# Differential-attention units: the rotated rows of queries and keys come by transfers instead of products with a matrix, and the value projection is cut into half blocks

## The reference, cut to what matters

```python
def apply_partial_rope(x, cos, sin):
    half = ROT_DIM // 2                       # 8
    x1, x2, xp = x[..., :half], x[..., half:ROT_DIM], x[..., ROT_DIM:]
    return jnp.concatenate([x1 * c - x2 * s, x2 * c + x1 * s, xp], axis=-1)
...
u = rms_norm(h, g_mix[l]) @ w_in[l]
qa = u[..., ...].reshape(B, S, DA_HEADS, 2, HEAD_DIM)     # 4 heads, 2 components each
ka = ...; va = ...
qa = apply_partial_rope(qa, cos, sin)
ka = apply_partial_rope(ka, cos, sin)
ya = diff_attention(qa, ka, va, lam, g_subln[l], lam_init)
```

## Time and profile before

| | |
|---|---|
| Time, median of 3 runs | 2294.36 us (2291.03 to 2294.76) |
| Profiled execution, its own time | 2291.01 us, with a span of 2289.2 us |
| Mean granted TensorE clock | 0.995 of full speed |
| TensorE busy | 2214.7 us, 97% of the span |
| VectorE busy | 1377.4 us, 60% |
| ScalarE busy | 952.1 us, 42% |
| GpSimd busy | 700.9 us, 31% |
| Differential units | 72.6 us to about 310 us of the span |

### The profile page before, as it was taken

The page is one execution under the profiler, slowest core; times in us unless marked ns, Lnnn a source line. Parts: engine busy times, 40 slices in busy tenths (PEclk is TensorE's granted clock), DMA queues, the critical chain, the costliest instruction groups (busy, mean ns, idle before and its releaser), DMA issues.

```text
span 2289.2 us, 36425 instructions
## 1 busy us (share of the span) xinstructions
PE 2214.7 (97%) x14780; PEld 1752.0 (77%) x14780; DVE 1377.4 (60%) x1775; ACT 952.1 (42%) x1688; POOL 700.9 (31%) x436
## 2 busy tenths in 40 slices
PE   7999999998999999999999999999999999999997
PEld 4777776665788888788888888888676777778885
DVE  6777857778676544584574575323508376567554
ACT  4444457777544232354234334233416412363321
POOL 2312212121211213274564565322231133122231
PEclk9999999999999999999999999999999999999998
DMA  3211101113131001111111110112220011100022
GB/s 134 74 56 56 47 19 56 56 47 129 50 138 54 29 27 39 45 47 56 56 55 44 57 64 29 54 55 92 77 73 19 19 38 38 40 20 13 4 111 83
DMA packets 38555, 125.80 MB, mean 55 GB/s; under 512 B 3856, under 2 KB 4368, under 8 KB 37776
## 3 DMA queue, kind: packets, MB, share of 16 engines
q1 hardware_dynamic: 33936, 103.30, 13.3%
q10 hardware_dynamic: 4480, 20.49, 2.3%
HBM read 114.34 MB, written 8.91 MB: 54 GB/s over the span
## 4 chain that ended last, share of the span: by engine, by line
PE 86%; DVE 6%; ACT 4%; issue 3%; POOL 1%; DMA 0%; ACTq 0%; DVEq 0%; POOLq 0%
PE PS L184 23%; PE PS L186 22%; PE PS L185 22%; PE PS L2305 2%; PE PS L776 2%; PE PS L753 1%; PE PS L1212 1%; PE PS L938 1%; PE PS L903 1%; PE PS L920 1%; DVE arena L1024 1%; PE PS L312 1%; PE PS L1915 1%; PE PS L1775 1%; PE PS L1788 1%
## 5 line engine op out<-in xcount | busy, mean ns | idle before, releaser
L233 POOL TENSOR_TENSOR w_hi<-w_raw,const 128x1024 fp32r<-128x1024 f32 x77 | 152.0, 1974 | 1096.6 <-PE PS L184 985.9
L184 PE MATMUL PS<-u_r,w_hi 128*128 128x512 f32 x1184 | 477.6, 403 | 9.0 <-DVE h L590 3.1
L186 PE MATMUL PS<-u_r,w_lo 128*128 128x512 f32 x1184 | 462.1, 390 | 0.0
L194 POOL TENSOR_TENSOR w_lo<-w_raw,w_hi 128x1024 fp32r<-128x1024 f32 (+1 forms) x143 | 330.7, 2313 | 323.2 <-ACT w_hi L190 308.3
L185 PE MATMUL PS<-arena_r,w_hi 128*128 128x512 f32 (+1 forms) x888 | 331.9, 374 | 0.0
L184 PEld LDWEIGHTS PS<-u_r,w_hi 128*128 128x128 f32 x1184 | 222.5, 188 | 62.0 <-DVE h_r L194 6.5
L186 PEld LDWEIGHTS PS<-u_r,w_lo 128*128 128x128 f32 x1184 | 222.4, 188 | 47.7
L184 PE MATMUL PS<-h_r,w_hi 128*128 128x512 f32 x512 | 207.8, 406 | 1.8 <-POOL w_lo L194 1.5
L186 PE MATMUL PS<-h_r,w_lo 128*128 128x512 f32 x512 | 200.2, 391 | 0.0
L185 PE MATMUL PS<-y_r,w_hi 128*128 128x512 f32 x512 | 199.5, 390 | 0.0
L1556 DVE TENSOR_TENSOR h<-h,PS 128x512 f32<-128x512 f32 x288 | 181.6, 683 | 21.6 <-PE PS L186 17.6
(11 more groups left out here) (434 smaller groups left out, 4280.4 us busy)
## 6 DMA issues: line engine op xcount, KB each, us to landing
w_raw<-in_w SPq DMA_DIRECT2D x174, 512.0 KB, 3.4
arena<-in_w SPq DMA_DIRECT2D x10, 512.0 KB, 5.0
h<-in_xT ACTq DMA_DIRECT2D x1, 4096.0 KB, 14.4
u<-parked_stream ACTq DMA_DIRECT2D x1, 4096.0 KB, 12.8
out<-arena SPq DMA_DIRECT2D x16, 256.0 KB, 2.0
parked_stream<-h ACTq DMA_DIRECT2D x6, 512.0 KB, 2.6
h<-in_xT SPq DMA_DIRECT2D x8, 256.0 KB, 6.7
h<-in_xT ACTq DMA_DIRECT2D x8, 256.0 KB, 8.8
```

Of the source, the lines that this page charges most:

```text
L184: first = pe.matmul(out, a[0], b[0], start=start, stop=False)
L186: return first, pe.matmul(out, a[1], b[0], start=False, stop=stop)
L194: return e.tensor_tensor(out, x, hi_part.bitcast(F), ALU.subtract)
L233: pool.tensor_tensor(out, src, cst("ones")[:, 0:1].broadcast_to([P, D]), ALU.mult).then_inc(S("w_high"), 1)
```

## The change

The `r` chunks and the matrix `rot` are gone. After the second half of a `q` or `k` chunk of a differential unit has been evacuated, ScalarE waits for that evacuation and issues four transfers inside SBUF of 8 partitions x 4 KB each, from the raw rows to `heads(w)`. The minus sign moves into the frequencies (negative for the first 8 features). Rows that no transfer writes are set to zero once, by four memsets on VectorE. `rope_dve` waits for the transfers of the unit. The values' two chunks are cut into half blocks, one half in each of the items 4 to 7; before, the first of them stood whole in item 5.

```diff
@@ constants
-                  ("ident", 128), ("rot", 128), ("masks", 192), ("blk64", 128),
+                  ("ident", 128), ("masks", 192), ("blk64", 128),
...
-            f[b + m] = np.float32(500000.0) ** np.float32(-(2.0 * (m % 8)) / 16.0)
+            f[b + m] = np.float32(500000.0) ** np.float32(-(2.0 * (m % 8)) / 16.0) * (1 if m >= 8 else -1)
@@ order of chunks
-        FIRST_CHUNKS = [("q", 0, 0), ("k", 0, 0), ("q", 0, 1), ("r", 0, 0), ("r", 0, 1), ("k", 0, 1), ("r", 0, 2), ("r", 0, 3),
-                        ("v", 0, 0), ("v", 0, 1), ("t", 0, 0), ("t", 0, 1)]
+        FIRST_CHUNKS = [("q", 0, 0), ("k", 0, 0), ("q", 0, 1), ("k", 0, 1), ("v", 0, 0), ("v", 0, 1), ("t", 0, 0), ("t", 0, 1)]
 
         def da_parts(i, s):
             w = i + 1
-            if s >= 6:
-                return ([(("ada", i, 0), None)] if s == 7 else []) + [(("v", w, 1), s - 6)] + ([(("t", w, 0), None)] if s == 7 else [])
-            o = [[("o", i - 1, h)] if i > 0 else [] for h in range(2)]
-            r = [[("r", w, n)] if w < N_DA else [] for n in range(4)]
-            whole = {0: ([("t", i, 1)] if i > 0 else []) + [("q", w, 0)], 1: [("q", w, 1)], 2: [("k", w, 0)] + o[0], 3: [("k", w, 1)] + o[1],
-                     4: r[0] + r[1], 5: r[2] + [("v", w, 0)] + r[3]}[s]
-            return [(c, None) for c in whole]
+            if s >= 4:
+                half = [(("v", w, s // 2 - 2), s % 2)]
+                return [(("ada", i, 0), None)] + half + [(("t", w, 0), None)] if s == 7 else half
+            o = [(("o", i - 1, s - 2), None)] if i > 0 and s >= 2 else []
+            t = [(("t", i, 1), None)] if i > 0 and s == 0 else []
+            return t + [(("qk"[s // 2], w, s % 2), None)] + o
@@ chunk_pe
-            elif what == "r":
-                pe.wait_ge(*chunk_done(("qk"[h // 2], w, h % 2)))
-                m = pe.matmul(b, cst("rot"), raw[:, h, :], start=True, stop=True)
@@ chunk_act
-            elif what == "r":
-                e = act.activation(heads(w)[h // 2][:, cols], b, ACT.Copy)
...
             e.then_inc(S("proj_evac"), 1)
+            if what in "qk" and h == 1 and w < N_DA:
+                act.wait_ge(*chunk_done(c))
+                for at in (0, 64):
+                    for lo, hi in ((0, 8), (8, 0)):
+                        act.dma_start(heads(w)[x][at + lo:at + lo + 8, :], raw_qk[x][at + hi:at + hi + 8, :]).then_inc(S("rotated_in"), 16)
@@ rope_dve
-            dve.wait_ge(*chunk_done(("r", w, 2 * x + 1)))
+            if x == 0:
+                dve.wait_ge(S("rotated_in"), 128 * (w + 1))
@@ VectorE, start of the kernel
+            for x in range(2):
+                dve.memset(heads(0)[x], 0.0)
             dve.tensor_scalar(gsub[:, :], vcol("g_subln"), 1.0 - LAM_INIT, None, ALU.mult)
...
+            for x in range(2):
+                dve.memset(heads(1)[x], 0.0)
             dve.wait_ge(S("ang_ready"), 3)
             for x in range(2):
                 rope_dve(dve, 0, x)
@@ ScalarE, before unit 0
-                if c == ("r", 0, 3):
+                if c == ("k", 0, 1):
                     act.wait_ge(S("ang_ready"), 1)
                     act.activation(sinT, ang, ACT.Sin).then_inc(S("ang_ready"), 1)
                     act.activation(cosT, posf, ACT.Sin, bias=cst("half_pi"), scale=-1.0).then_inc(S("ang_ready"), 1)
@@ TensorE, before unit 0
-                if c[0] == "r":
+                if c == ("t", 0, 0):
                     pe.wait_ge(S("const_late"), 16)
```

More of the change, by code:

```diff
@@ L51, in constants @@
     put("blk64", (i[:, None] // 64) == (i[None, :] // 64))
[L52 to L57, removed]
     short = np.concatenate([np.eye(P), NEG * (i[None, :] > i[:, None]), NEG * (i[None, :] >= i[:, None])], axis=1).astype(np.float32)
@@ L2955, in _ @@
                 dve.tensor_tensor(lamt[:, x:x + 1], vec[:, o + 2 * x:o + 2 * x + 1], vec[:, o + 2 * x + 1:o + 2 * x + 2],
-                                  ALU.mult).then_inc(S("lam_prod"), 1)
+                                  ALU.mult).then_inc(S("lam_a"), 1)
+            for x in range(2):
+                dve.memset(heads(0)[x], 0.0)
             dve.tensor_scalar(gsub[:, :], vcol("g_subln"), 1.0 - LAM_INIT, None, ALU.mult)
@@ L2982, in _ @@
             dve.tensor_tensor(lamt[:, 4:5], lamt[:, 3:4], lamt[:, 2:3], ALU.subtract).then_inc(S("lam_a"), 1)
-            dve.wait_ge(S("lam_a"), 2)
+            dve.wait_ge(S("lam_a"), 4)
             dve.tensor_scalar(lamt[:, 5:6], lamt[:, 4:5], LAM_INIT, None, ALU.subtract).then_inc(S("lam_a"), 1)
-            dve.wait_ge(S("lam_a"), 3)
+            dve.wait_ge(S("lam_a"), 5)
+            for x in range(2):
+                dve.memset(heads(1)[x], 0.0)
             dve.wait_ge(S("ang_ready"), 3)
@@ L3388, in _ @@
             pe.wait_ge(S("const_in"), 16)
-            pe.wait_ge(S("lam_prod"), 2)
+            pe.wait_ge(S("lam_a"), 3)
             pe.matmul(bank(0)[:, 0:2], cst("ones"), lamt[:, 0:2], start=True, stop=True).then_inc(S("lam_sum"), 1)
```

## The result

The change made the kernel slower: 2306.16 us (median of 5 runs, 2302.41 to 2308.8) against 2294.36 us before (5 runs, 2291.03 to 2295.3). The ratio is 1.0053, with a 95% interval of 1.0042 to 1.0065. That is 12 us where I forecast 4, and above the range of 2290 to 2302. The profiled execution took 2306.16 us, with a span of 2304.4.

A forecast was written before the change was run, and what follows sets the result against it. TensorE, busy 97% of the span, was taken as the bound, with VectorE as much so in items 5 to 7. Terms -1.3 + 5.7 + 0.1 - 0.4 = +4.1 us, set on 2292.8, gave 2297 us, range 2290 to 2302.

The forecast's parts named there:

- Before unit 0: Ahead of the first unit: ScalarE begins the sine earlier and the rotary passes end earlier; -1.3 us, bounds -2.2 and 0.
- Item 1 of units 0 to 2: Four issues ahead of the copy make TensorE stand 1.9 us per unit, uncovered; +5.7 us, ends 3.3 and 6.6.
- Items 3 to 7 of units 0 to 2, with the stall of item 3: Late copy in item 3 and fewer products afterwards, with VectorE deciding; -0.1, +0.1, +0.1 us, about nothing.
- Unit 3: No rot products or transfers; half of v in item 4 fills part of a TensorE wait; -0.4 us, bounds -0.8 and 0.4.
- The split's move: GpSimd's split starts in item 4 beside VectorE's weights, stretching L833 and L838 to about 5 us; L713, L715 take 1.2.
- the sine: Ahead of unit 0: ScalarE, free earlier, finishes sine and cosine at 61.6 us, not 63.06; transfers land just in time, 61.4.
- Issues in a row back up: Rival for ScalarE's issues: 0.6 us each, item 1 costs 6.6 us; +5.9, 2299 us; chance 0.25.
- Cheap issues: Rival for ScalarE's issues: 0.33 us each, item 1 costs 3.3 us; -0.7, 2292 us; chance 0.15.
- the products simply go: Rival: issues take well under 0.2 us each, so copies are not delayed; -6 or more, 2286 us; chance 0.05.
- VectorE does not bind: Rival: the split misses item 4's weights, items 3 to 7 give back 5.2 us; -1.2, 2292 us; chance 0.13.

The follow-up runs named there:

- e2: The changed kernel with the same transfers issued by ScalarE after the last copy of items 1 and 3, not right after the evacuation; 2290.42 us, ratio 0.9988.
- e5: The changed kernel with two issues in a group in place of four, so one component of a head is not rotated rightly; 2295.88 us, ratio 1.0012.
- e3: The changed kernel with the first chunk of the values whole in item 5 again, transfers unchanged; 2310.84 us, ratio 1.0072.
- e8: e2 with the first chunk of the values whole in item 5 again; 2297.78 us, ratio 1.0017.
- e7: The changed kernel without transfers and with the rotary step of units 1 to 3 in one pass in place of three; 2287.25 us, ratio 0.9974.
- e1: The changed kernel with its 32 transfers left out, so the rotation is not computed; 2289.05 us, ratio 0.9981.
- e4: The kernel before, rot products included, plus the 32 transfers at the changed kernel's place, to rows nobody reads; 2324.77 us, ratio 1.0124.
- e6: The changed kernel with all 32 transfers issued by SyncE's queue between its weight panel loads, none on ScalarE; 2289.59 us, ratio 0.9982.
- e12: e6 with 16 small unused products at the very start of TensorE's work, none ahead of unit 0; 2287.10 us, ratio 0.9969.
- e11: e6 with 8 small unused products at the very start of TensorE's work and 8 ahead of unit 0; 2285.59 us, ratio 0.9965.

## Why the prediction was wrong

By its own terms, measured in the profiled executions:

| Term | Predicted | Measured |
|---|---|---|
| Before unit 0 | -1.3 | -0.8 |
| Item 1 of units 0 to 2 | +5.7 | +11.2 (4.2 + 4.3 + 2.7) |
| Items 3 to 7 of units 0 to 2, with the stall of item 3 | +0.1 | +3.4 (1.1 + 1.2 + 1.1) |
| Unit 3 | -0.4 | +0.6 |
| Sum at 310 us | +4.1 | +14.4 |

**The step that failed** is the stall of item 1: "It stands 1.9 us ... Three units: 5.7 us, with 3.3 and 6.6 as the ends". Place, mechanism and the work queued behind were right, and so was that nothing covers it. Its size was wrong twice. An issue took 0.63 us, not 0.52, so TensorE stood 2.5 us and not 1.9 (2.0 by the prediction's own times), and the next item came 2.7 us late where the clock stayed up; the bound of 0.61, from a row of 64 partitions, was itself too low for 8 partitions. That is 2.4 us over three units. The rest, 3.1 us, is the clock: two of the three waits came with a stretch at 1.2 GHz worth 1.6 us each. The prediction has no term for that, and no rival; it priced idle time of TensorE as idle time. e2 shows that both parts go when the wait vanishes, and e5 that the wait shrinks with the issues.

**Items 3 to 7** were said to come to about nothing because VectorE hides the late copy. e5 shows such hiding with 1.5 us of lateness. The four issues made the wait 2.05 us in unit 0 and 2.85 in units 1 and 2, and at all three places the clock fell. This is the second step that failed: +3.4 us in place of +0.1. e2 differs from the changed kernel in the place of the issues alone and needs 37.5 us in unit 1 where the latter needs 40.0. How the 2.5 us divide between the wait and the clock I have not separated. One place hints at the clock: in unit 0 of e3 the wait was 2.06 us, the clock stayed up, and items 3 to 7 needed 0.3 us more than in e8; in units 1 and 2, with waits of 2.85 and a fall each, 2.1 and 3.1 more.

**Behind 310 us** the prediction has no term. The profile gains 2 us there and loses 3, most of it at the two places where every kernel with fewer matmuls loses. At the medians the change is 11.8 us and not 15.2, since the profiled execution of before is 3.4 us below its median.

**What was right.** The split's move: VectorE's weights of item 4 and the rotary step now read, beside the earlier trace rows:

```profile
108.57 1.76 DVE L826 TENSOR_SCALAR arena<-arena,er,lamt 128x640 f32<-128x640 f32 x1
110.36 2.87 DVE L831 SCALAR_TENSOR_TENSOR arena<-arena,er 128x640 f32<-128x640 f32 x1
...
117.12 1.22 DVE L706 TENSOR_TENSOR y<-y,arena 128x1024 f32<-128x1024 f32 x1
118.38 1.23 DVE L708 TENSOR_TENSOR y<-y,arena 128x1024 f32<-128x1024 f32 x1
```

L826 and L831 are stretched to 4.6 us together, and L706 and L708 are undisturbed. The rule of the Trainium skill that was cited for it (SBUF — State Buffer, "SBUF: two separate sides") agrees: the loss moved with the split. Its size did not stay the same, as the prediction had drawn from the rule; it went from 3.8 to 3.1 us. That the half blocks are still worth 5 to 7 us, as e3 and e8 show, is not explained by that: in e8 most of the added waits are for the exponentials, since item 4 has no chunk. The two were not separated. Ahead of unit 0 the sine was not the gate, as I had it, but the landing of the last transfers, which let the rotary step begin at 64.1 us. The two groups ahead of unit 0 held ScalarE for 3.3 and 3.0 us and not 2.1, and the last rows were there 4.8 us after the start of their issue and not 3.7. It still gained 0.8 us of the 1.3 forecast.

**The rivals.** "Issues in a row back up" was the nearest, with 0.63 us for each, but they do not back up: each of the 16 to `y` took 0.63 to 0.66 (the first issue of all, at 51.5 us, took 1.25). It gave 2299 us since it too lacked the clock. "Cheap issues" and "the products simply go" are refuted by the issue time. "VectorE does not bind" fails by its condition, since the split did meet the weights of item 4; yet e7 puts no more than 0.8 us a unit down to the rotary step. e1 shows what "the products simply go" would have given: 0.19% faster. Of the 13.8 us of the products 5.2 are there at 310 us in its profile, the rest being hidden behind other waits, and 2.6 of these are lost again between 2070 and 2190 us.

The Trainium skill (DMA: Bandwidth & Descriptors, "Issuing engines are not separate DMA queues") says that the time to initiate a transfer is "usually small relative to the DMA itself". Here one issue took 0.63 us, against 3.7 us from issue to landing in the nearest row, which does not contradict it; but four in a row held their engine for 2.6 us. Where the issuing engine is awaited, this is the cost that counts.

## What to carry to other kernels

When an instruction stream issues a transfer, price the issue as an instruction of that engine and look at what stands behind it in order; the same 32 issues cost 17 us ahead of a copy that TensorE awaited, and right behind it 1.4 us, with overlapping intervals. Price a wait of a busy TensorE with its clock: in the profiles waits of 0.9 to 1.6 us in the differential units came without a fall of the clock, and most of those of about 2.5 us with one, which cost 1.6 us more. When one profile stands for a kernel, compare its time and mean clock with those of the other executions. And try the parts of a change apart, because here a good half (half blocks of the values, 5 to 7 us) was hidden under a misplaced one.

## What the runs showed of the hardware that I had not expected

- An issue of an 8-partition transfer inside SBUF took 0.63 us on ScalarE and 0.62 us on SyncE, about twice the 0.33 us of a 128-partition one to memory. Smaller was not cheaper; the two differ in their destination too, and which of the two makes the price was not separated.
- Of the 32 waits of 1.8 to 2.9 us that TensorE had ahead of and in the differential units, in all profiles, 22 came with a fall of the granted clock to 1.2 GHz. In those of the changed kernel, e3 and e4 it fell at all six of 2.85 us, at six of the nine of 2.5 us in item 1, and at one of the three of 2.05 us in item 3. Ahead of unit 0 it fell after 1.9 us in e6, e7 and e12, but not after 1.9 in e1, 2.3 in the changed kernel and 2.4 in e5. At the 12 waits of 0.9 to 1.6 us it did not fall. A fall cost 1.6 us where TensorE had work queued.
- These lengths are no rule for other places: at 1814 us of the kernel before TensorE waited 1.1 us, then ran matmuls of 16 partitions, and the clock fell (0.51 in the stretch):

```profile
1814.52 1.98 PE L1897 MATMUL PS<-arena,y 16*128 16x512 f32 x4 [1.10 <-ACT arena L1962]
1816.80:1820.30 3.50, 3.50 (x10) 2.76 (x9) 0.00 (x0) 3.40 (x4) 3.21 (x2) 0.51 0.00 0
```

- With 16 small products that nobody reads in the wait ahead of unit 0, TensorE's clock stayed at 2.4 GHz (granted clock of the stretch 1.00 against 0.91). With half of them, in e11, it did too. There is one profile of each, and in e1 the clock stayed up after the same wait without them.
- With 32 matmuls fewer near the start TensorE lost 2.0 to 3.2 us at two places some 1900 us later, in all nine profiles; in the four with as many matmuls as before, 0.0 to 0.5 us.
